# Late parts of u, squared chunks summed on GpSimd, a piecewise end and a chunk-wise start, in a four-layer decoder step

## The chip, the cores and the metric

The kernel runs on one core of one Trainium2 chip. The metric is the device time of one execution in microseconds (us). All times and rows here are of that one core.

## The reference, cut to what matters

One inference step of a decoder trunk. There are 1040 prompt columns and 32 sample columns, 1072 in all, each a vector of 1024 numbers. The trunk is: an attention and RWKV mixer, an MLP, a pooling mixer, an MLP. Each of the four is sandwiched between two RMS norms:

```
def rms_norm(x, g): return x * rsqrt(mean(x*x, -1) + 1e-6) * g
def channel_mixer(x, g_pre, g_post, w_up, w_down):      # the MLP, hidden width 4096
    h = rms_norm(x, g_pre)
    y = square(relu(h @ w_up)) @ w_down
    return x + rms_norm(y, g_post)
# pooling mixer: h = rms_norm(x); windows of 2, 4, 8, 16 columns, mean minus h,
#                a 256x256 product per group, then x + rms_norm(y, g_post)
```

The last MLP's x is the output y. Other outputs (latent rows, states) are written by stages that the change does not touch.

## The kernel before, in words

Features lie on the partitions, 128 at a time: x and y are tiles [128, 8 chunks, 1072 columns]. The columns are cut into three tiles of 358, 358 and 356. Products are made in float32r in three passes (`three_passes`, L222): weight and input are each split into a rounded head and a tail, and head*head, head*tail and tail*head are added up in PSUM.

**The first stage** (`project`, 20 slabs of w_in): ScalarE makes the heads of the input x chunk by chunk (L330), VectorE the tails (L395), GpSimd the tails of the weight slabs (L383). TensorE multiplies slab 0 with the column tiles 0, 1 and 2 in turn. Before each it waits for `x_tail`, which counts tiles: all eight chunks of that tile.

**The last stage** (`dense`) holds the output product (24 slots), the two MLPs and the pooling mixer between them. An MLP of one layer is two passes over its weights, the first for the column tiles 0 and 1, the second for tile 2 alone, so there are four passes of 64 slabs, 256 slabs of 512 KB. A pass has 8 blocks (fb) of 8 slabs, named here r0 to r7. r0 to r3 are up-slabs: 24 matmuls per column tile give 128 hidden rows in a PSUM bank; VectorE takes max(.,0)*rstd into `rl` (L2450), ScalarE squares it (L2274) and copies the rounded head into `u` (L2276), VectorE makes the tail (L2461, counter `u_tail`). r4 to r7 are down-slabs: each holds two output chunks (half 0 and 1) and multiplies all four parts of u, 12 matmuls per half and tile; VectorE adds the result to y (L2456; L2454 in the first block). Each slab is loaded by SP (L2021), its head is made by ScalarE (L2168) and its tail by VectorE (L2289) one slab ahead; there are two buffers, and the head of slab i+1 waits until TensorE is through slab i-1. A PSUM bank is written again only when VectorE has emptied it (`emptied`). One-tile slabs have 24 matmuls, two-tile slabs 48.

Each engine's program is written out by hand. Per slab i: ScalarE does head(i+1), `chains`, then the two activations of u; VectorE does tail(i+1), `chains`, then the emptying of slab i's products, then the tail of u; TensorE does slab i's products, then `chains`.

**The chains** are the norms, residuals and the pooling mixer. They hang on slots: job j of column tile t begins at slab start+o. A norm is: four squares of two chunks each (`square`, L2175, ScalarE, into sq[0] and sq[1] in turn), four `sums` (L2054, TensorE, 8 fp32 matmuls per part that the profile counts as 16), `root` (ScalarE), `invert` (VectorE, a reciprocal), `spread` (L2064, TensorE), and then `post` on VectorE: y times the rate (L2301) and x + y (L2308), two chunks a slot. `BETWEEN` places the four norms of one column tile between the two layers: POST_F (after the first MLP), PRE_M (before pooling), POST_M (after it), FFN1 (before the second MLP, with heads L2191 and tails L2321 of its input). Tile 0 starts at slab 65, tile 1 at 94 (both in the second pass, one tile a slab), tile 2 at 129 (third pass). `h_one`, `window_sums`, `pool` and `pool_product` (L2074) are the pooling mixer. `ENDING` places the last norm of tiles 0 and 1 in the fourth pass; that of tile 2 comes after slab 255. SP stores y in three pieces, one per column tile, each when its eight chunks are final; it also stores the pooling state (`pool_p`, `pool_s`) after it has issued slab 144.

The order of the work is fixed by these lists and the semaphores; there is no planner. GpSimd has no work in `dense`.

## Time and profile before

| | us |
|---|---|
| median of 3 timed runs (lowest, highest) | 3288.15 (3286.95, 3291.96) |
| the profiled execution: time | 3278.4 |
| its span | 3276.7 |
| TensorE matmuls busy | 2961.1 (90%) |
| VectorE busy | 1496.3 (46%) |
| ScalarE busy | 988.4 (30%) |
| GpSimd busy | 243.3 (7%) |

The span goes from the first to the last instruction of the profiled execution. The first stage lies before about 275 us, the last stage from 1436 us on; its four passes begin at about 1564, 2087, 2428 and 2972 us, and the last slab's products end at 3254. In a timeline row the second number is the length in us, `x24` is how many instructions the row merges, and the bracket is the idle time of the engine before the first of them, with what ended it. TensorE's granted clock (PEclk) is 1.00 at 2.4 GHz and 0.50 at 1.2 GHz.

### The profile page before, as it was taken

How to read it: one execution, taken by the hardware profiler on the slowest of the kernel's cores; microseconds unless marked ns; L12 is line 12 of the kernel's file. 1: busy time of each engine (PE TensorE's matmuls, PEld its weight loads, DVE VectorE, ACT ScalarE, POOL GpSimd, SP SyncE). 2: the span in 40 equal slices, each digit the busy share in tenths (PEclk: the TensorE clock that was granted, in tenths of full speed). 3: DMA queues.
4: the chain of work that ended last, by engine and by line, in shares of the span. 5: the costliest groups of instructions: out<-in, count | busy, mean ns of one | idle time of the engine just before them, and what ended most of it. 6: DMA issues, size and time to landing. Idle time of an engine off the chain costs nothing.

```text
span 3276.7 us, 70726 instructions
## 1 busy us (share of the span) xinstructions
PE 2961.1 (90%) x30941; PEld 2617.1 (80%) x30941; DVE 1496.3 (46%) x2569; ACT 988.4 (30%) x1817; POOL 243.3 (7%) x282
## 2 busy tenths in 40 slices
PE   7997888887888879989999999998999999999997
PEld 7996676664555556656999999988899899999896
DVE  3554444443343344413544434566655453445554
ACT  3102333321333334313322222334342232223332
POOL 1122222210000004300000000000000000000000
PEclk9997776866899889989999999999999999999998
DMA  3110000001000007730222222323342722223344
GB/s 121 40 39 28 5 4 4 4 5 57 1 8 10 0 13 233 220 124 1 78 65 68 68 65 65 90 90 98 97 97 65 59 65 65 65 65 97 116 123 131
DMA packets 92721, 216.85 MB, mean 66 GB/s; under 512 B 26833, under 2 KB 49778, under 8 KB 91666
## 3 DMA queue, kind: packets, MB, share of 16 engines
q1 hardware_dynamic: 86290, 193.71, 20.5%
q0 software_dynamic: 6144, 18.88, 1.9%
q8 instruction: 233, 3.82, 0.5%
q14 instruction: 54, 0.44, 0.0%
HBM read 205.11 MB, written 7.45 MB: 65 GB/s over the span
## 4 chain that ended last, share of the span: by engine, by line
PE 49%; DVE 4%; ACT 1%; DMA 1%; issue 1%; DVEq 0%; ACTq 0%
PE ps L222 44%; PE ps L2133 4%; PE ps L2074 1%; PE ps L2054 1%; DMA ds_raw<-w_mlp_dram 1%; DVE ds_rl L2450 1%; ACT ds_split L2168 1%; DVE ds_y L2301 1%; DVE ds_split L2289 1%; DVE ds_x L2308 1%; DVE ds_u L2461 0%; ACT ds_rl L2274 0%; PE ps L2064 0%; ACT ds_u L2276 0%; DVE ds_h L2321 0%
## 5 line engine op out<-in xcount | busy, mean ns | idle before, releaser
L222 PE MATMUL ps<-ds_u,ds_split 128*128 128x358 f32 (+1 forms) x4608 | 779.2, 330 | 57.1 <-DVE ds_u L2461 52.3
L222 PEld LDWEIGHTS ps<-ds_u,ds_split 128*128 128x128 f32 x4608 | 761.7, 190 | 69.7 <-issue 66.5
L222 PE MATMUL ps<-ds_h,ds_split 128*128 128x358 f32 (+1 forms) x4608 | 777.0, 328 | 4.2 <-DVE ds_y L2456 2.3
L222 PEld LDWEIGHTS ps<-ds_h,ds_split 128*128 128x128 f32 x4608 | 759.2, 189 | 13.1 <-issue 5.5
L2168 ACT CAST ds_split<-ds_raw 128x1024 fp32r<-128x1024 f32 x256 | 268.1, 1047 | 641.7 <-PE ps L222 623.3
L2289 DVE TENSOR_TENSOR ds_split<-ds_raw,ds_split 128x1024 fp32r<-128x1024 f32 x256 | 313.6, 1225 | 143.6 <-ACT ds_split L2168 143.5
L2456 DVE TENSOR_TENSOR ds_y<-ds_y,ps 128x358 f32<-128x358 f32 (+1 forms) x336 | 175.2, 524 | 281.9 <-PE ps L222 281.4
L222 PE MATMUL ps<-h,in_split 128*128 128x358 f32 (+1 forms) x1440 | 240.7, 328 | 16.8 <-DVE h L395 16.8
L222 PEld LDWEIGHTS ps<-h,in_split 128*128 128x128 f32 x1440 | 236.7, 189 | 18.3 <-issue 14.8
L2274 ACT ACTIVATE ds_rl<-ds_rl 128x358 f32<-128x358 f32 (+1 forms) x192 | 96.5, 503 | 497.9 <-DVE ds_rl L2450 497.9
L2450 DVE SCALAR_TENSOR_TENSOR ds_rl<-ps,ds_rstd 128x358 f32<-128x358 f32 (+1 forms) x192 | 101.5, 529 | 280.7 <-PE ps L222 277.2
L2461 DVE TENSOR_TENSOR ds_u<-ds_rl,ds_u 128x358 fp32r<-128x358 f32 (+1 forms) x192 | 101.3, 528 | 112.0 <-ACT ds_u L2276 112.0
L1441 PE MATMUL ps<-pa_PT,pa_V 128*64 128x128 f32 (+1 forms) x720 | 95.4, 280 | 60.4 <-DVE pa_PT L1546 42.1
L1441 PEld LDWEIGHTS ps<-pa_PT,pa_V 128*64 128x64 f32 x720 | 76.6, 145 | 78.5 <-issue 73.1
L1510 DVE TENSOR_REDUCE pa_mx<-ps 128x1 f32<-128x128 f32 (+8 forms) x72 | 58.3, 810 | 150.3 <-PE ps L1392 150.3
L2133 PE MATMUL ps<-z,ds_wout 128*128 128x358 f32 (+1 forms) x384 | 120.0, 471 | 4.3 <-DMA ds_wout<-w_out_dram 4.3
L1635 POOL DMA_DIRECT2D sa_C<-pool_dram x128 | 69.2, 541 | 579.1 <-issue 574.4
L2133 PEld LDWEIGHTS ps<-z,ds_wout 128*128 128x128 f32 x384 | 72.7, 192 | 45.7 <-DMA ds_wout<-w_out_dram 4.5
L2276 ACT CAST ds_u<-ds_rl 128x358 fp32r<-128x358 f32 (+1 forms) x192 | 94.4, 492 | 6.1
L1771 DVE COPY z<-ps 128x512 f32<-128x512 f32 (+1 forms) x80 | 51.0, 638 | 94.4 <-PE ps L1671 94.1
L1388 PE MATMUL ps<-pa_KT,pa_QT 96*128 96x512 f32 (+3 forms) x192 | 91.2, 589 | 0.0
L1671 PEld LDWEIGHTS ps<-const,sa_C 128*128 128x128 f32 x576 | 64.4, 144 | 29.8 <-issue 22.2
(326 smaller groups left out, 3330.5 us busy)
## 6 DMA issues: line engine op xcount, KB each, us to landing
ds_raw<-w_mlp_dram SPq DMA_DIRECT2D x256, 512.0 KB, 3.6
sa_C<-pool_dram SPq DMA_DIRECT2D x128, 144.0 KB, 3.1
sa_C<-pool_dram POOLq DMA_DIRECT2D x128, 144.0 KB, 3.3
in_raw<-w_in_dram SPq DMA_DIRECT2D x20, 512.0 KB, 3.6
ds_x<-xc_dram SPq DMA_DIRECT2D x1, 4288.0 KB, 18.8
ds_wout<-w_out_dram SPq DMA_DIRECT2D x8, 512.0 KB, 6.6
z<-xc_dram SPq DMA_DIRECT2D x2, 1432.0 KB, 9.6
y_dram<-ds_x SPq DMA_DIRECT2D x2, 1432.0 KB, 9.8
```

The source lines that it names most:

```text
L222: last = self.nc.tensor.matmul(out, w[:, a, k, m], rhs[:, b, rk, at:at + c], start=(start and n == 0), stop=(stop and n == 2))
L1388: mm(ps[0:n, bank + at // 512, 0:c], q, KT[:, e, at:at + c], start=True, stop=True)
L1441: last = mm(ps[rr(e), 6 + u % 2, 0:n], V[0:m, kb, rr(e)], PT[0:m, u % 2, kb, 0:n], start=(kb == 0), stop=(kb == i))
L1635: engine.dma_start(C[:, t % SLOTS, j:j + 1, :], io["pool"][bass.ds(page, 1)].rearrange("a p m -> p a m")).then_inc(pages_in[lane][t % SLOT ...
L2133: end = mm(ps[:, slot % 2, 0:wide(t)], wout[m][:, k, :], z[:, (Z_K + k if k < PAIRS else Z_R + k - PAIRS), cols(t)], start=(k == 0), stop= ...
L2168: nc.scalar.copy(split[i % 2][:, 0, :, :], raws[i % 2][:, :, :]).then_inc(g["slab_heads"].sem, 1)
L2274: nc.scalar.activation(rl[:, e % 2, 0:wide(n)], rl[:, e % 2, 0:wide(n)], ACT.Square).then_inc(g["u_squared"].sem, 1)
L2276: nc.scalar.copy(u[:, 0, r, u_cols(n)], rl[:, e % 2, 0:wide(n)]).then_inc(g["u_head"].sem, 1)
L2289: tt(split[i % 2][:, 1, :, :], raws[i % 2][:, :, :], split[i % 2][:, 0, :, :].bitcast(F32), ALU.subtract).then_inc(g["slab_tails"].sem, 1)
L2450: stt(out=rl[:, e % 2, 0:c], in0=ps[:, bank, 0:c], scalar=0.0, in1=rstd[:, cols(n)], op0=ALU.max, op1=ALU.mult).then_inc(g["emptied"].sem, 1)
L2456: tt(y[:, m, cols(n)], y[:, m, cols(n)], ps[:, bank, 0:c], ALU.add).then_inc(g["emptied"].sem, 1)
L2461: tt(u[:, 1, r, u_cols(n)], rl[:, e % 2, 0:wide(n)], u[:, 0, r, u_cols(n)].bitcast(F32), ALU.subtract).then_inc(g["u_tail"].sem, 1)
```

## The change

- **u late.** In the first down-slab of a block (r4) TensorE first runs the passes over the parts 0 to 2 of u for all halves and tiles (9 matmuls each), and only then, after waiting for the fourth part, the last 3 of each. In between, all banks stay open.
- **Sums between the layers.** For the 12 norms of `BETWEEN` (jobs 6 to 17) ScalarE squares part 0 into sq[0] and parts 1 to 3 into sq[1]; GpSimd adds the chunks (7 adds a job, 128 x 358 each), and TensorE makes one set of 4 matmuls where it made four sets of 8. ScalarE's squares of parts 2 and 3 wait for GpSimd's adds of the part before. The slots are spread out: tile 1 starts at slab 97 and tile 2 at 131, later steps come one to four slots later, and the pooling state is stored after slab 151.
- **The end.** TensorE runs the sums of the last norm's parts 0 to 2 behind the products of slabs 253, 254 and 255; ScalarE's squares for it stand behind its last head. GpSimd adds the odd chunks of x, VectorE the even ones, and SP stores tile 2 in four pieces of two chunks.
- **The start.** In slab 0 TensorE waits per chunk of x, not per tile.

The diff, cut to its core:

```diff
@@ project, tensor
-                            if m == 0:
-                                pe.wait_ge(g["x_tail"].sem, g["x_tail"].at(n + 1))
                             for k in range(KC):
+                                if m == 0:
+                                    pe.wait_ge(g["x_tail"].sem, g["x_tail"].at(KC * n + k + 1))
@@ dense
-        BETWEEN = {0: OUT_SLOTS + FIRST[0, 1] + 1, 1: OUT_SLOTS + FIRST[0, 1] + 30, 2: OUT_SLOTS + FIRST[1, 0] + 1}
+        BETWEEN = {0: OUT_SLOTS + FIRST[0, 1] + 1, 1: OUT_SLOTS + FIRST[0, 1] + 33, 2: OUT_SLOTS + FIRST[1, 0] + 3}
+        def by_pool(j):
+            return 6 <= j < 18
@@ sync
-                        if i == FIRST[1, 0] + 16:
+                        if i == FIRST[1, 0] + 23:
-                    for t in range(3):
+                    for t in range(2):
...
+                    for pair in range(KC // 2):
+                        sp.wait_ge(g["x_new"].sem, g["x_new"].at(KC * POST_NUMBER[LAST(2)] + pair + 1))
+                        sp.wait_ge(g["x_late"].sem, g["x_late"].at(pair + 1))
+                        sp.dma_start(io["y"][:, 2 * pair:2 * pair + 2, cols(2)], x[:, 2 * pair:2 * pair + 2, cols(2)]).then_inc(g["stored"].sem, 16)
@@ tensor, sums
+                        if by_pool(j):
+                            pe.wait_ge(g["added"].sem, g["added"].at(added_at(j, 3)))
+                            for q, at, c in quarters(wide(tile_of(j))):
+                                end = mm(ps[32 * q:32 * q + 32, 6, 0:c], self.c("ones", hi=32), sq[0][:, 0, at:at + c], start=True, stop=True)
+                            end.then_inc(g["summed"].sem, 1)
+                            return
@@ tensor, slots o of BETWEEN: before -> after
-  sums POST_F 0,1 (4 parts)  spread 2   sums PRE_M 4..7   spread 8   pool_product 11,13,15,17  sums POST_M 13,15,17,19  spread 20  sums FFN1 22..25  spread 26
+  sums POST_F 2 (one set)    spread 3   sums PRE_M 9      spread 10  pool_product 13,15,17,19  sums POST_M 22           spread 23  sums FFN1 29      spread 30
@@ tensor, products of a down-slab
+                            for k in range(UP - 1 if r == UP else UP):
+                                end = self.three_passes(ps[:, bank, 0:c], split[i % 2], UP * half + k, slice(0, P), u, k, u_cols(n).start, c, k == 0, k == UP - 1)
+                            if r > UP:
+                                end.then_inc(g["product"].sem, 1)
+                        if r == UP:
+                            for q, half, n, bank, before in uses[i]:
+                                if half == 0:
                                     pe.wait_ge(g["u_tail"].sem, g["u_tail"].at(up_number[i - 1, n] + 1))
+                                self.three_passes(ps[:, bank, 0:wide(n)], split[i % 2], UP * half + UP - 1, slice(0, P), u, UP - 1, u_cols(n).start, wide(n),
+                                                  False, True).then_inc(g["product"].sem, 1)
+                        if i >= N_SLABS - 3:
+                            sums(LAST(2), i - N_SLABS + 3)
                         chains(OUT_SLOTS + i)
-                    for o in range(3):
-                        ending(2, o)
+                    sums(LAST(2), 3)
+                    spread(LAST(2))
@@ scalar, square
+                        if part >= 2:
+                            if by_pool(j):
+                                act.wait_ge(g["added"].sem, g["added"].at(added_at(j, part - 1)))
+                        if by_pool(j) and part:
+                            nc.scalar.activation(sq[1][:, :, 0:wide(t)], src[:, 2 * part:2 * part + 2, cols(t)], ACT.Square).then_inc(g["squared"].sem, 1)
+                            return
@@ scalar, slots: PRE_M squares 4..7 -> 5..8, POST_M squares 13..19 -> 15..21, FFN1 heads and squares 22..25 -> 25..28; after the loop:
+                    for part in range(4):
+                        act.wait_ge(g["emptied"].sem, g["emptied"].at(done_slab(N_SLABS - 4 + part)))
+                        square(LAST(2), part, y)
+                    root(LAST(2))
@@ new
+                @block.gpsimd
+                def _(pool):
+                    add = nc.gpsimd.tensor_tensor
+                    for j in range(6, 18):
+                        c = wide(tile_of(j))
+                        for part in range(4):
+                            pool.wait_ge(g["squared"].sem, g["squared"].at(4 * j + part + 1))
+                            if part:
+                                pool.wait_ge(g["added"].sem, g["added"].at(added_at(j, part - 1)))
+                                add(sq[1][:, 0, 0:c], sq[1][:, 0, 0:c], sq[1][:, 1, 0:c], ALU.add).then_inc(g["added"].sem, 1)
+                                pool.wait_ge(g["added"].sem, g["added"].at(added_at(j, part) - 1))
+                            with_part = sq[1][:, 0, 0:c] if part else sq[0][:, 1, 0:c]
+                            add(sq[0][:, 0, 0:c], sq[0][:, 0, 0:c], with_part, ALU.add).then_inc(g["added"].sem, 1)
+                    n = POST_NUMBER[LAST(2)]
+                    for k in range(1, KC, 2):
+                        pool.wait_ge(g["scaled"].sem, g["scaled"].at(KC * n + k + 1))
+                        add(x[:, k, cols(2)], x[:, k, cols(2)], y[:, k, cols(2)], ALU.add).then_inc(g["x_late"].sem, 1)
@@ vector, post
+                            if j == LAST(2) and k % 2:
+                                continue
@@ vector, slots: POST_F post 3..6 -> 4..7, h_one 9..12 -> 11..14, windows 10,12,14,16 -> 12,14,16,18, pool 11,13,15,17 -> 13,15,17,19, POST_M post 21..24 -> 24..27, FFN1 tails 22..25 -> 25..28
```

## Rows read from the trace of the kernel before

**Rows 1.** The four passes as stretches: length, busy PE PEld DVE ACT POOL, PEclk, DMA share, GB/s.
```profile
1560.00:2087.00 527.00, 516.87 (x3228) 511.57 (x3227) 221.10 (x347) 138.10 (x211) 0.00 (x0) 1.00 0.22 69
2087.00:2427.50 340.50, 310.77 (x2178) 288.78 (x2177) 221.09 (x338) 135.82 (x200) 0.00 (x0) 0.96 0.32 98
2427.50:2971.50 544.00, 533.03 (x3394) 521.33 (x3393) 250.17 (x424) 147.63 (x228) 0.00 (x0) 0.99 0.31 66
2971.50:3255.00 283.50, 261.76 (x1683) 254.87 (x1681) 159.00 (x226) 100.97 (x138) 0.00 (x0) 0.99 0.41 124
```

**Rows 2.** Waits: who waited for whom, us in total, times, longest.
```profile
PE ps L222 <- DVE ds_u L2461: 52.3, 31, 4.1
```

**Rows 3.** Timeline, a two-tile pass, where up turns to down (start, length, idle before).
```profile
1732.64 4.53 PE L222 MATMUL ps<-ds_u,ds_split 128*128 128x358 f32 x26 [1.15 <-DVE ds_u L2461]
```

**Rows 4.** Timeline, a one-tile pass, where up turns to down.
```profile
3168.11 0.53 DVE L2450 SCALAR_TENSOR_TENSOR ds_rl<-ps,ds_rstd 128x356 f32<-128x356 f32 x1
...
3170.41 15.78 PE L222 MATMUL ps<-ds_u,ds_split 128*128 128x356 f32 x96 [2.33 <-DVE ds_u L2461]
...
3170.68 1.23 DVE L2289 TENSOR_TENSOR ds_split<-ds_raw,ds_split 128x1024 fp32r<-128x1024 f32 x1 [0.42 <-ACT ds_split L2168]
...
3172.61 0.53 DVE L2456 TENSOR_TENSOR ds_y<-ds_y,ps 128x356 f32<-128x356 f32 x1 [0.71 <-PE ps L222]
```

**Rows 5.** Timeline, two down slabs of the second pass, one sums part between.
```profile
2287.85 4.14 PE L222 MATMUL ps<-ds_u,ds_split 128*128 128x356 f32 x24
...
2292.37 4.14 PE L222 MATMUL ps<-ds_u,ds_split 128*128 128x356 f32 x24
```

**Rows 6.** One line's instructions (min/median/max ns), and one GpSimd instruction of the timeline.
```profile
L1285 POOL TENSOR_TENSOR rw_bonus_v<-rw_bonus_v,rw_lnb x9: 1260/1288/1350, 310.2 to 713.5; 128x512 f32<-128x512 f32 x8, 64x512 f32<-64x512 f32 x1
...
L395 DVE SCALAR_TENSOR_TENSOR h<-z,vec,h x24: 577/586/2352, 10.6 to 25.9; 128x358 fp32r<-128x358 f32 x16, 128x356 fp32r<-128x356 f32 x8
...
20.22 2.41 POOL L383 TENSOR_TENSOR in_split<-in_raw,in_split 128x1024 fp32r<-128x1024 f32 x1 [10.09 <-ACT in_split L324]
```

**Rows 7.** Timeline and one stretch, second pass, where updates of x crowd VectorE.
```profile
2122.74 1.08 DVE L2301 SCALAR_TENSOR_TENSOR ds_y<-ds_y,vec,ps 128x358 f32<-128x358 f32 x2
...
2123.96 0.97 DVE L2308 TENSOR_TENSOR ds_x<-ds_x,ds_y 128x358 f32<-128x358 f32 x2
...
2221.61 0.52 DVE L2450 SCALAR_TENSOR_TENSOR ds_rl<-ps,ds_rstd 128x356 f32<-128x356 f32 x1
...
2228.43 0.52 DVE L2450 SCALAR_TENSOR_TENSOR ds_rl<-ps,ds_rstd 128x356 f32<-128x356 f32 x1
...
2281.94 5.53 PE L222 MATMUL ps<-ds_u,ds_split 128*128 128x356 f32 x24 [4.07 <-DVE ds_u L2461]
...
2141.00:2152.00 11.00, 6.93 (x30) 6.66 (x29) 8.47 (x14) 2.77 (x4) 0.00 (x0) 0.69 0.33 100
```

**Rows 8.** DMA issues (KB, us to landing) and timeline, third pass, rows of the pooling state.
```profile
pool_s_dram<-ds_full SPq DMA_DIRECT2D x1, 480.0 KB, 32.1
...
2576.27 1.04 ACT L2168 CAST ds_split<-ds_raw 128x1024 fp32r<-128x1024 f32 x1 [15.36 <-DMA ds_raw<-w_mlp_dram]
```

**Rows 9.** Timeline and DMA issues, the end.
```profile
3254.82 2.92 ACT L2175 ACTIVATE ds_sq<-ds_y 128x712 f32<-128x712 f32 x4 [7.22 <-DVE ds_y L2456]
...
3261.95 1.08 DVE L2301 SCALAR_TENSOR_TENSOR ds_y<-ds_y,vec,ps 128x356 f32<-128x356 f32 x2 [2.11 <-PE ps L2064]
...
3268.79 0.97 DVE L2308 TENSOR_TENSOR ds_x<-ds_x,ds_y 128x356 f32<-128x356 f32 x2
...
y_dram<-ds_x SPq DMA_DIRECT2D x1, 1424.0 KB, 6.4
```

**Rows 10.** Timeline, the start.
```profile
14.83 9.79 PE L222 MATMUL ps<-h,in_split 128*128 128x358 f32 x48 [14.83 <-DVE h L395]
...
20.67 5.85 DVE L395 SCALAR_TENSOR_TENSOR h<-z,vec,h 128x356 fp32r<-128x356 f32 x8 [1.96 <-ACT h L330]
...
26.58 8.10 PE L222 MATMUL ps<-h,in_split 128*128 128x356 f32 x48 [1.95 <-DVE h L395]
```

More of the change, by code:

```diff
@@ L462, in _ @@
                     chain.close()
-            for n, events in (("product", 3 * NZ), ("emptied", 3 * NZ), ("slab_heads", NZ), ("slab_tails", NZ), ("loaded", 16), ("late_in", 64), ("x_head", 3 * KC), ("x_tail", 3)):
+            for n, events in (("product", 3 * NZ), ("emptied", 3 * NZ), ("slab_heads", NZ), ("slab_tails", NZ), ("loaded", 16), ("late_in", 64), ("x_head", 3 * KC), ("x_tail", 3 * KC)):
                 g[n].passed(events)
@@ L1946, in dense, with added_at @@
         PREPARED = {(layer, t): 3 * layer + t for layer in range(2) for t in range(3)}
+        def by_pool(j):
+            return 6 <= j < 18
+        events = [0]
+        for j in range(21):
+            events.append(events[-1] + (1 if by_pool(j) else 4))
+        ADDS = 7
+        def added_at(j, part):
+            return ADDS * (j - 6) + 2 * part + 1
         def cols(t):
@@ L2424, in chains @@
-                            if 22 <= o < 26:
-                                tails(1, t, range(2 * (o - 22), 2 * (o - 22) + 2))
+                            if 11 <= o < 15:
+                                h_one(t, range(2 * (o - 11), 2 * (o - 11) + 2))
+                            if o in (12, 14, 16, 18):
+                                windows[t] = window_sums(t, (o - 12) // 2)
+                            if o in (13, 15, 17, 19):
+                                pool(t, (o - 13) // 2, *windows[t])
@@ L2426, in chains @@
+                            if 25 <= o < 29:
+                                tails(1, t, range(2 * (o - 25), 2 * (o - 25) + 2))
                         for t, start in ENDING.items():
```

115 lines of the change are left out of this document (51 added, 64 removed).

## The prediction

> **What bounds the kernel now.** I read the busy time by stretch first, since the change touches four places that have different limits. In all four MLP passes TensorE is the engine that sets the time, at a granted clock near 1.00: it is busy for 516.9 of 527, 310.8 of 340.5, 533.0 of 544 and 261.8 of 283.5 us [rows 1]. So in the passes with two tiles little is left to gain beside work taken off TensorE, and in the passes with one tile 30 and 22 us are idle. The view of waits says for what: 52.3 us, in 31 waits, for the last tail of u, by far the longest item of TensorE [rows 2]. There is one such wait in each of the 32 blocks. In a two-tile pass it is 1.15 us [rows 3], in an undisturbed one-tile pass 2.33 us [rows 4], in the second pass up to 4.07 us [rows 7].
>
> Why it is 2.33: the last up-product ends just before VectorE's 3168.11 row; then come VectorE, two activations and VectorE again, until TensorE starts at 3170.41 [rows 4]. Meanwhile ScalarE and VectorE prepare the next slab: its tail runs from 3170.68 to 3171.91. This loop (empty the bank, two activations, head, tail) is some 3.85 us long against 24 matmuls of 15.78/96 = 0.164 us, 3.94 us. So in one-tile up-slabs TensorE and the loop are tied: whatever delays VectorE or ScalarE there comes out as a stall, and in two-tile slabs (twice as long) it does not.
>
> **Part 1, u late, two tiles (passes 1 and 3).** 36 matmuls (5.9 us) now stand ahead of the first use of u's last part, so the wait of 1.15 us goes. What is late next? The next slab's tail is ready some 3.9 us after the last up-product, and the first bank's last 3 matmuls end 1.5 us before the slab's end, while VectorE needs 0.53 us to empty it: nothing. 16 blocks x 1.15 = 18.4 us gained.
>
> **Part 2, u late, one tile.** 18 matmuls (2.95 us) cover the 2.33. But now r4 ends at about 3168.07 + 3.94 = 3172.0, half 0 and half 1 end 0.5 us apart at its very end, and r5 needs half 0's bank. On VectorE the tail of the next slab stands ahead of the emptying and lasts till 3171.91; then 0.53 us of emptying: r5 starts at 3172.55, against 3170.41 + 3.94 = 3174.35 before. 1.8 us a block are gained, 0.5 lost to the new wait. In pass 4 six blocks are like this; in the first two the post of tiles 0 and 1 stands in r4 on VectorE (2.1 us, as in [rows 7]) ahead of the emptying, and eats nearly all of it: 0.5 each. Pass 4: 6 x 1.8 + 1 = 12 us.
>
> **Part 3, sums.** One part of sums between two slabs makes 4.52 us from start to start [rows 5] where 3.94 is the slab: 0.6 us a part. Of 4 parts per norm one set of half the size stays (0.45 us by that row: most of it is the change-over); where two parts stood together (POST_F) the change-over was shared. I count 7 us per column tile (four norms: 1.5, 1.9, 1.8, 1.8), 21 for all. For tile 2 in pass 3 nothing else is near the limit: 7 us.
>
> **Part 4, the pooling state's store.** Its transfer takes 32.1 us and the weight slab behind it came so late that ScalarE idled 15.36 us waiting for a DMA [rows 8]; at TensorE this cost some 5 us beside the slow clock after it. Moved from slab 144 to 151, it goes out while slab 148 is worked on; between then and the need for slab 152 lie two slabs with a pooling product, as before one and a half. I take 4 us gained (bounds: 0, if the slab is as late as before, and 7).
>
> **Part 5, pass 2 (tiles 0 and 1 between the layers, one tile a slab).** Gained: u late 8 x 1.8 = 14 us; sums 14 us, but not all of it counts. Where x is updated, VectorE needs 1.23 (slab tail) + 1.08 + 0.97 [rows 7] + 2 x 0.53 = 4.3 us a down-slab, more than TensorE's 3.94: the sums of PRE_M and FFN1 stood in that shadow. I keep 8 us. Tile 1's first update (slots 97 to 100, which are r1 to r4) ended in the wait of 4.07 us and a stretch on the slow clock (5.53 us for 24 matmuls) [rows 7]; it moves to r5, r6, r7 and r0, which I put at 4 us gained.
> Lost: (a) POST_M's update and FFN1's heads, squares and tails move from r6, r7, r0, r1 (tile 0) and r3 to r6 (tile 1) to r1 to r5 for both. There the loop is 0.53 + 1.0 + 1.05 + 1.23 + 2.05 + 1.1 us, about 7, which the trace shows: 6.82 us between two L2450 with both in between [rows 7]. TensorE then stalls some 1 + 3 + 2 us in r2 to r4, and in r5 once more (4 us), because VectorE has not emptied r4's banks: some 11 us a tile, with the clock lowered after each longer stall; a window with such a wait stood at 0.69 between the levels of 1.2 and 2.4 GHz (0.50 and 1.00) [rows 7], so 13. Today the two tiles lose about 4 each by the same count. Net 9 a tile, 18 us. (b) In POST_F, ScalarE's fourth square waits for the two adds of the third. An add of 128 x 358: one of 512 columns takes 1.29 us, one of 1024 takes 2.41 [rows 6], a slope of 1.12 per 512, so 0.95 us. Two adds are 1.9 us in front of an up-slab's activations: 1.8 us x 2 tiles = 3.5 us. (c) The adds against VectorE: a VectorE instruction with both inputs in SBUF took 2352 ns in place of 586 when GpSimd's 2.41 us instruction had begun 0.45 us before it [rows 6]; it waited for the end. 56 adds of 0.95 us in this pass; where they come, VectorE spends about a third of its time in such forms (slab tails, u tails, x + y), so a third of them hit, half an add each, and half of that reaches TensorE: 56 x 1/3 x 0.47 x 1/2 = 4 us; bounds 0 and 56 x 0.95 = 53. I round (a) to (c) to 23 to 25 us against 26 gained. To this comes that the pooling windows meet up-slabs a little more kindly (the 4 us window no longer in r1 but in r3, where 0.5 us of slack now lies): 3. Net 5 us gained; this is the least certain term, and I give it -12 to +26.
> The Trainium skill, "SBUF — State Buffer", section "Who interferes with whom", says that a VectorE instruction with two SBUF inputs and a GpSimd one that reads SBUF shut each other out for their whole length. By that rule, the trace agrees (2352 ns against 586), and with every add on the path it would turn the sum as in the last rival.
>
> **Part 6, the end.** After the last product: emptying, 4 squares (2.92 us from 3254.82), sums, root, spread, post from 3261.95, the last x + y ending at 3269.76, a store of 1424 KB that lands in 6.4 [rows 9]. Now three squares leave that line: 2.2 us gained. But square 0 stands on ScalarE behind head(255), which waits for the products of slab 253, and TensorE's sums behind slab 253 wait for it: 0.05 + 1.05 + 0.8 + 0.1 = 2.0 us of stall, and two parts of sums at 0.6 are now in line: 3.2 us lost. Post: VectorE drops 4 x 0.48 = 1.9 us, GpSimd's last add ends 0.95 after it; the last of four stores is a quarter: the three quarters before it (at 360 GB/s 3 us) are gone. 1.9 - 0.95 + 3 = 4 us gained. End: 3 us (0 to 5).
>
> **Part 7, the start.** TensorE now follows the tails chunk by chunk. Tile 2's tails end at 20.67 + 5.85 = 26.52, and its 24 matmuls were then all to come [rows 10]; now 3 are: 21 x 0.163 = 3.4 us. What comes behind it (sums, root) waits on TensorE, not on a load. 3.4 us (bounds 0 and 3.9).
>
> **Sum.** 18.4 + 12 + 7 + 4 + 5 + 3 + 3.4 = 53 us. 3278.4 - 53 = 3225 for an execution like the profiled one. The median of the timed runs is 3288.15, 10 us above it; I take the difference off the median: 3235 us.
>
> **Rivals.**
> A. The later slots cost nothing in pass 2 (ScalarE and VectorE catch up in the slack that u late opens). For it: tile 0's update of today, half of it in up-slabs, loses only some 4 us. Against: the 6.82 us loop. (a) falls to nothing: 53 + 18 = 71, 3217 us.
> B. Pass 2 is crowded more than I count, because each stall brings the slow clock and the locks hit in the same slots: 20 us more, 3255 us.
> C. The wait for u's last part is replaced in full, by the bank that r5 needs or by the next slab's tail. For it: the tail ends only 0.1 us before r4 does [rows 4]. Against: the same row ends it in time. Then 18.4 + 14 + 12 = 44 go, and 9 are left: 3279 us.
> D. Slower than before: the lock between GpSimd and VectorE. 84 adds in `BETWEEN`, 0.95 us each; if each pushed VectorE back by its whole length on the path, 80 us, less the 4 counted: 3235 + 76 = 3311 us. It decides from 0.67 us on the path per add (57/84). Against: a third of the adds fall into pass 3, where VectorE is busy for 250 of 544 us [rows 1] and has time to give, and most of its work in pass 2 reads PSUM and one tile only.
>
> **Chances.** Forecast 0.52, A 0.19, B 0.16, C 0.06, D 0.05, and 0.02 that it all cancels. Within 0.2% means within 6.6 us, about what a measurement of this kernel can tell from no change. Faster: forecast, A, B and C but for its upper end: 0.92. Same: 0.03. Slower: 0.05. The forecast's own range is 3220 to 3250; with A's and B's centres, the term of pass 2 (-12 to +26) and the bounds of parts 4, 6 and 7 it is 3206 to 3264.
>
> **What would show it.** Waits of TensorE for L2461 gone in passes 1, 3 and 4, and in pass 4 r4 plus r5 with a wait of about 0.5 us for the bank (L2456). Passes 1 to 4 shorter by 9, 5, 20 and 12 us. In pass 2 L2450 at distances of 5.5 to 7 us in slots 89 to 92 and 121 to 124 with waits of TensorE for VectorE of 2 to 4 us in r4 and r5. A TensorE stall of 2 us behind slab 253 for ScalarE's square. The last store landing in 3.3 us. GpSimd's adds at 0.95 us; single L2308 or L2289 lengthened by up to that. It would be wrong if pass 2 (340.5 us) came out shorter than 320 or longer than 350 us, or if passes 1 and 3 kept a wait at r4 or r5.

## The result: 3238.82 us against 3287.55, and the profile after

Timed beside each other, the changed kernel takes 3238.82 us (median of 4 runs, 3234.22 to 3243.11) and the kernel before 3287.55 (3286.38 to 3291.96): a ratio of 0.9849 with an interval of 0.9831 to 0.9867, or 48.7 us less. 3235 was forecast. In the profiled executions it is 3234.22 against 3278.4 us, 44.2 less, where the sum of the prediction has 53.

The four MLP passes and the stretch after slab 252, by the view of windows (us; columns as in [rows 1]: length, busy us and count of PE, PEld, DVE, ACT and POOL, granted clock, DMA share, GB/s):

```profile
1565.80:2079.00 513.20, 511.44 (x3216) 509.95 (x3217) 220.29 (x346) 137.59 (x210) 0.00 (x0) 1.00 0.22 70
2079.00:2415.50 336.50, 299.49 (x1729) 277.67 (x1727) 234.01 (x338) 136.55 (x201) 60.52 (x56) 0.96 0.32 99
2415.50:2946.50 531.00, 523.78 (x3171) 518.57 (x3170) 254.77 (x425) 147.03 (x228) 30.47 (x28) 0.99 0.33 67
2946.50:3219.00 272.50, 263.13 (x1731) 253.97 (x1729) 158.31 (x226) 103.44 (x141) 0.00 (x0) 1.00 0.41 129
```

The first pass has 1.8 us of idle left in 513, so it stands at what its matmuls need. The second pass still has 37 us idle, more than before (30), although it is shorter: what was taken off TensorE there did not all come off the time.

TensorE's waits from 1500 us to the end (us in total, times, longest):

```profile
PE ps L222 <- DVE ds_y L2511: 21.9, 17, 7.2
PE ps L2094 <- DVE ds_y L2436: 9.6, 5, 3.0
PE ps L222 <- DVE ds_split L2342: 8.8, 8, 2.7
PE ps L222 <- DVE ds_y L2509: 5.7, 5, 1.8
PE ps L222 <- DVE ds_rl L2505: 4.7, 2, 2.6
PE ps L2074 <- ACT ds_sq L2208: 2.9, 2, 1.9
```

The item of 52.3 us for u's last tail [rows 2] is gone (its line would be L2516). In its place stand waits for a bank to be emptied (L2511), for the next slab's tail (L2342) and for the windows of the pooling (L2436): 53.6 us in these six rows, of which the first five have 34.8 in the second pass, and the longest single wait, 7.2 us, stands in the third.

For what follows I cut each profile at the start of the first product of slabs 0, 64, 128, 192 and 252 (starts of L222 in the timeline) and take the differences. "Start" runs to the beginning of the last projection product of the first stage; "middle" is the stretch between it and slab 0, in which all kernels here are the same.

| kernel | start | middle | pass 1 | pass 2 | pass 3 | pass 4 to slab 252 | from there to the end |
|---|---|---|---|---|---|---|---|
| before | 271.0 | 1293.4 | 522.9 | 340.4 | 544.0 | 266.8 | 38.2 |
| changed | 267.1 | 1298.6 | 513.2 | 336.6 | 531.1 | 251.7 | 34.2 |
| changed, second profile (e11) | 267.8 | 1290.6 | 513.2 | 336.7 | 528.3 | 251.6 | 34.5 |
| e1 only u late | 271.1 | 1303.4 | 513.2 | 329.2 | 534.6 | 251.5 | 37.6 |
| e2 old slots, TensorE sums | 267.3 | 1301.8 | 514.8 | 329.9 | 533.1 | 251.5 | 33.8 |
| e3 new slots, TensorE sums | 268.2 | 1308.6 | 514.8 | 326.3 | 535.7 | 251.5 | 35.9 |
| e4 old slots, GpSimd adds | 267.1 | 1304.2 | 513.3 | 348.7 | 529.5 | 251.5 | 34.3 |
| e5 pool_s in pieces | 266.8 | 1289.0 | 513.2 | 335.8 | 520.9 | 251.6 | 35.2 |
| e6 square first | 267.3 | 1284.1 | 514.8 | 333.4 | 527.9 | 251.4 | 31.7 |
| e7 adds doubled | 267.1 | 1295.7 | 513.3 | 354.4 | 528.2 | 251.4 | 35.2 |
| e8 GpSimd for tile 2 only | 269.1 | 1287.4 | 513.3 | 326.6 | 528.3 | 251.5 | 34.6 |
| e9 e8 + pieces + square first | 267.2 | 1299.4 | 514.8 | 328.9 | 520.9 | 251.6 | 31.7 |
| e10 e9 + GpSimd in two norms | 267.0 | 1303.3 | 514.8 | 323.8 | 520.9 | 251.5 | 32.1 |

This table says how far a single profile can be trusted. The middle, in which no kernel differs, runs from 1284 to 1309 us, so whole times of single executions differ by up to 25 us for nothing; the passes repeat to some 3 us (e11 against the changed kernel: 0.0, 0.1, 2.8, 0.1; pass 2 of e3, e8 and e9, which have the same order in it: 326.3, 326.6, 328.9; pass 2 of the changed kernel's order in its two profiles, e5 and e6: 336.6, 336.7, 335.8, 333.4). The two values of pass 1, 513.2 and 514.8, differ in one slab, the sixth (8.8 or 10.3 us), for a reason not looked into. The steps are judged by the passes. Changed against before they give -3.9, -9.7, -3.8, -12.9, -15.1 and -4.0, together -49.4; the middle gave 5.2 back.

### The profile page after: what moved, and what is told of

The parts are those of the page before. It is cut to its first block, busy times and chain, and to the rows that moved or that the text cites. A ratio compares the mean times of both kernels' runs of the same rounds, so it can differ in the third digit from the quotient of the medians.

```text
span 3232.5 us, 69489 instructions
## 1 busy us (share of the span) xinstructions
PE 2944.9 (91%) x30269; PEld 2605.6 (81%) x30269; DVE 1512.2 (47%) x2565; ACT 988.2 (31%) x1817; POOL 338.7 (10%) x370
## 3 DMA queue, kind: packets, MB, share of 16 engines
q1 hardware_dynamic: 86338, 193.71, 20.6%
## 4 chain that ended last, share of the span: by engine, by line
PE 46%; DVE 4%; ACT 2%; issue 1%; DMA 1%; POOL 0%; ACTq 0%; DVEq 0%; POOLq 0%
PE ps L222 41%; PE ps L2150 4%; ACT ds_split L2195 1%; DVE ds_split L2342 1%; DMA ds_raw<-w_mlp_dram 1%; PE ps L2094 1%; DVE ds_y L2354 1%; DVE ds_x L2363 1%; ACT ds_rl L2307 1%; PE ps L2084 1%; DVE ds_rl L2505 1%; PE ps L2074 0%; DVE ds_h L2376 0%; DVE ds_wa L2415 0%; DVE ds_y L2511 0%
## 5 line engine op out<-in xcount | busy, mean ns | idle before, releaser
L222 PE MATMUL ps<-ds_u,ds_split 128*128 128x358 f32 (+1 forms) x4608 | 779.5, 329 | 30.9 <-DVE ds_y L2511 14.3
L222 PEld LDWEIGHTS ps<-ds_u,ds_split 128*128 128x128 f32 x4608 | 760.6, 190 | 42.7 <-issue 21.6
L222 PE MATMUL ps<-ds_h,ds_split 128*128 128x358 f32 (+1 forms) x4608 | 776.4, 328 | 10.9 <-DVE ds_y L2511 7.6
L222 PEld LDWEIGHTS ps<-ds_h,ds_split 128*128 128x128 f32 x4608 | 759.7, 189 | 20.1 <-DVE ds_split L2342 13.5
L2342 DVE TENSOR_TENSOR ds_split<-ds_raw,ds_split 128x1024 fp32r<-128x1024 f32 x256 | 315.1, 1231 | 144.6 <-ACT ds_split L2195 144.6
L2511 DVE TENSOR_TENSOR ds_y<-ds_y,ps 128x358 f32<-128x358 f32 (+1 forms) x336 | 171.8, 524 | 235.8 <-PE ps L222 234.6
L222 PE MATMUL ps<-h,in_split 128*128 128x358 f32 (+1 forms) x1440 | 241.7, 329 | 12.0 <-DVE h L395 12.0
L222 PEld LDWEIGHTS ps<-h,in_split 128*128 128x128 f32 x1440 | 237.4, 190 | 13.8 <-POOL in_split L383 10.9
L2505 DVE SCALAR_TENSOR_TENSOR ds_rl<-ps,ds_rstd 128x358 f32<-128x358 f32 (+1 forms) x192 | 101.5, 529 | 264.6 <-PE ps L222 257.5
L2327 POOL TENSOR_TENSOR ds_sq<-ds_sq 128x358 f32<-128x358 f32 (+1 forms) x48 | 54.4, 1134 | 993.8 <-ACT ds_sq L2208 991.0
L2516 DVE TENSOR_TENSOR ds_u<-ds_rl,ds_u 128x358 fp32r<-128x358 f32 (+1 forms) x192 | 102.2, 532 | 115.3 <-ACT ds_u L2309 115.3
## 6 DMA issues: line engine op xcount, KB each, us to landing
ds_x<-xc_dram SPq DMA_DIRECT2D x1, 4288.0 KB, 18.8
```

What stands on the lines that cost most here:

```text
L222: last = self.nc.tensor.matmul(out, w[:, a, k, m], rhs[:, b, rk, at:at + c], start=(start and n == 0), stop=(stop and n == 2))
L2342: tt(split[i % 2][:, 1, :, :], raws[i % 2][:, :, :], split[i % 2][:, 0, :, :].bitcast(F32), ALU.subtract).then_inc(g["slab_tails"].sem, 1)
L2505: stt(out=rl[:, e % 2, 0:c], in0=ps[:, bank, 0:c], scalar=0.0, in1=rstd[:, cols(n)], op0=ALU.max, op1=ALU.mult).then_inc(g["emptied"].sem, 1)
L2511: tt(y[:, m, cols(n)], y[:, m, cols(n)], ps[:, bank, 0:c], ALU.add).then_inc(g["emptied"].sem, 1)
L2516: tt(u[:, 1, r, u_cols(n)], rl[:, e % 2, 0:wide(n)], u[:, 0, r, u_cols(n)].bitcast(F32), ALU.subtract).then_inc(g["u_tail"].sem, 1)
```

## The experiments

**e1, u late alone.** The kernel before, with only TensorE's order in r4 changed:

```diff
-                                for k in range(UP):
+                            for k in range(UP - 1 if r == UP else UP):
...
+                                self.three_passes(..., UP * half + UP - 1, slice(0, P), u, UP - 1, ..., False, True).then_inc(g["product"].sem, 1)
```

> The kernel before with the late use of u's last part alone. Theory: the wait of 1.15 us goes in the 16 two-tile blocks and 1.8 us net in the one-tile blocks, so passes 1 and 3 lose 9 to 10 us each, pass 4 12 to 15, pass 2 14 or more, 50 us in all: about 3237. Rival (a new wait takes its place where ScalarE and VectorE are crowded): pass 2 moves by less than 6 us, and the sum is 35 to 40 us, about 3250.

Measured: 3245.32 us (3242.21 to 3246.00) against 3280.22, ratio 0.9896 (0.987 to 0.9921). By passes 9.7, 11.2, 9.4 and 15.3 us, 45.6 in all; the 35 of the medians hold the unsteady middle too. Passes 1 and 4 are where the whole change has them, so nothing else of the change acts there. Pass 2 gains 11.2: below the 14 that the prediction and the theory had, and above the 6 of the rival. It is 7.4 us more than the whole change gains there (4.3 by e6's profile of the same pass). What the change adds to pass 2 beside this is therefore a loss.

**e2 and e3, slots and sums apart.** e2 is the changed kernel with the old slots of `BETWEEN` (and the pooling state's store behind slab 144) and TensorE's four parts of sums; e3 keeps the new slots and the new place of the store, with TensorE's sums.

```diff
-            return 6 <= j < 18
+            return False
...
-        BETWEEN = {0: OUT_SLOTS + FIRST[0, 1] + 1, 1: OUT_SLOTS + FIRST[0, 1] + 33, 2: OUT_SLOTS + FIRST[1, 0] + 3}
+        BETWEEN = {0: OUT_SLOTS + FIRST[0, 1] + 1, 1: OUT_SLOTS + FIRST[0, 1] + 30, 2: OUT_SLOTS + FIRST[1, 0] + 1}
```

The first two lines are in both, the last two in e2 alone; the slots of the single steps, which follow from them, are left out here.

> The changed kernel without anything between the layers: TensorE makes all sums, in the slots of before, the pooling state is stored after slab 144. u late, the end and the start stay. Theory (the spread-out slots cost in pass 2 what the sums taken off TensorE give, and the later store costs 3 to 4 us in pass 3): pass 2 within 5 us of the changed kernel's 336.6, pass 3 longer than its 531.1 by 7 us of sums less 3.5 of the store, 534 to 535; whole time within 6 us of the changed kernel's 3239. Rival (GpSimd's adds carry a good part of the gain): pass 2 and 3 together longer by 15 us or more, 3255.

> The changed kernel with its new slots, but TensorE makes all sums, in four parts, and GpSimd adds none. Theory: in pass 3 the 7 us of sums come back whole (531.1 to 538); in pass 2 only what did not stand in VectorE's shadow, 8 us, less what GpSimd's adds cost there (the wait of ScalarE in POST_F 3.5 us and lengthened VectorE instructions 10 us in sum, about half on the path): within 4 us of the changed kernel's 336.6. Rival (the adds are free and the sums count in full): pass 2 longer by 12 to 14 us, about 350. Rival (the lock weighs more than the sums): pass 2 shorter by 5 us or more.

Measured: e2 3232.42 us, ratio 0.9854 (0.9828 to 0.9881); e3 3227.03 (3219.11 to 3242.84), ratio 0.9831 (0.9802 to 0.986). In whole times neither can be told from the changed kernel; in pass 2 both can: 329.9 and 326.3 against 336.6 (333.4 to 336.7 in the four profiles with this pass 2). e2 was to stay within 5 us of it and e3 within 4; both are shorter by more, and for e3 that is its second rival, by which the lock weighs more than the sums. So the expected net loss by the new slots is not there, and GpSimd's adds, which I had as a gain, cost 10 us with the new slots (5 to 10 over all profiles of the two orders).

**e4, old slots with GpSimd's adds,** for the three norms whose old slots leave them time:

```diff
-            return 6 <= j < 18
+            return 6 <= j < 18 and (j - 6) % 4 > 0
```

> The changed kernel with the slots of before; GpSimd adds the squares of three of the four norms between the layers (PRE_M, POST_M, FFN1), TensorE keeps POST_F's sums, the pooling state is stored after slab 144. Theory (the new slots put POST_M's update and FFN1's heads and tails of both tiles into up-slabs, at 9 us a tile): pass 2 shorter than the changed kernel's 336.6 by 10 to 18 us, about 322; whole time about 3225. Rival (the crowd is the same wherever it stands): pass 2 within 5 us of 336.6.

Measured: 3245.35 us (3237.82 to 3250.22), ratio 0.9887 (0.9859 to 0.9916); pass 2 at 348.7, longer by 12.1 than the changed kernel, where my theory had it shorter. That refutes the theory outright: with GpSimd's adds the new slots are better by 12.1 us; with TensorE's sums they are no worse (e3, e8 and e9 have 326.3 to 328.9, e1 and e2, the two kernels with the old slots, 329.2 and 329.9: 0.3 to 3.6 us, hardly more than the passes repeat to). The adds cost 5 to 10 us in the new slots (56 adds) and 18.8 in the old (42 adds). TensorE's waits in pass 2, first of e3, then of the changed kernel, then of e4:

```profile
PE ps L222 <- DVE ds_y L2514: 7.6, 7, 2.7
PE ps L2074 <- ACT ds_sq L2211: 7.5, 6, 2.0
PE ps L2094 <- DVE ds_y L2439: 3.1, 4, 1.2
```

```profile
PE ps L222 <- DVE ds_y L2511: 10.3, 8, 3.8
PE ps L2094 <- DVE ds_y L2436: 9.6, 5, 3.0
PE ps L222 <- DVE ds_split L2342: 8.8, 8, 2.7
PE ps L222 <- DVE ds_rl L2505: 4.7, 2, 2.6
```

```profile
PE ps L222 <- DVE ds_y L2512: 14.3, 8, 4.1
PE ps L2094 <- DVE ds_y L2437: 11.3, 6, 3.2
PE ps L2068 <- POOL ds_sq L2328: 9.5, 3, 6.1
```

With TensorE's sums, 7.5 us are waits for ScalarE's squares; with GpSimd's adds these are gone and VectorE is late instead, in its windows, tails and emptying. In e4 TensorE waits for GpSimd itself on top.

**e5, the pooling state's store in eight pieces,** one chunk of 60 KB behind each of eight slabs:

```diff
+                        if FIRST[1, 0] + 20 <= i < FIRST[1, 0] + 28:
+                            k = i - FIRST[1, 0] - 20
...
+                            sp.dma_start(io["pool_s"][:, k], full[:, k, :, DS:KEPT + DS]).then_inc(g["pool_out"].sem, 16)
...
-                            sp.dma_start(io["pool_s"], full[:, :, :, DS:KEPT + DS]).then_inc(g["pool_out"].sem, 16)
```

> The changed kernel with the pooling state's store cut into eight pieces, one behind each of the weight slabs 148 to 155, in place of one transfer after slab 151. Theory (the one transfer of 8192 small rows holds up the weight slab behind it): slabs 151 and 152 of pass 3 take 15.5 and 10.7 us in the changed kernel and 7.9 to 8.0 here, pass 3 shorter by 8 to 10 us, 522. Rival (the small rows cost the same wherever they stand, since each piece of some 4 us delays its slab): the loss is spread over slabs 149 to 156 and pass 3 stays within 3 us of 531.1.

Measured: 3214.19 us in one run, beside 3277.76 of the kernel before. Pass 3 takes 520.9 us, 10.2 less than in the changed kernel's first profile, 7.4 less than in its second and 7.0 less than in e6. Issues (KB each, us to landing) and ScalarE's wait, changed kernel, around slab 151:

```profile
pool_s_dram<-ds_full SPq DMA_DIRECT2D x1, 480.0 KB, 35.0
...
2622.20 1.04 ACT L2195 CAST ds_split<-ds_raw 128x1024 fp32r<-128x1024 f32 x1 [20.63 <-DMA ds_raw<-w_mlp_dram]
...
2625.09 16.16 PE L222 MATMUL ps<-ds_h,ds_split 128*128 128x358 f32 x80 [7.22 <-DVE ds_y L2511]
```

and the same issue in e9, which stores it in the same pieces:

```profile
pool_s_dram<-ds_full SPq DMA_DIRECT2D x8, 60.0 KB, 6.5
```

In e5 ScalarE has no wait for a DMA in this stretch. Slabs 151 and 152 took 15.52 and 10.72 us in the changed kernel and take 8.15 and 7.92, which is the 10.2 us of the pass. The other 62 slabs of the pass take 504.84 us in the changed kernel, in e11, in e6 and in e5 alike: all that differs between profiles of this pass stands in these two slabs. The row of TensorE names VectorE's emptying, but VectorE waited for ScalarE and ScalarE for the load: the releaser named last isn't the cause.

**e6, the square of part 0 ahead of the last head:**

```diff
+                        if i == N_SLABS - 2:
+                            act.wait_ge(g["emptied"].sem, g["emptied"].at(done_slab(N_SLABS - 4)))
+                            square(LAST(2), 0, y)
                         if i + 1 < N_SLABS:
                             head(i + 1)
```

> The changed kernel with ScalarE's first square of the last norm ahead of its last head, head(255). Theory (TensorE waits behind slab 253 for a square that stands behind that head): slab 253 takes 6.46 us in the changed kernel and 4.5 here, the end as a whole 1.9 to 2.0 us less. Rival (the wait is for the emptying of y or for the sums themselves): slab 253 stays above 6 us, or slab 254 takes what 253 gives.

Measured: 3212.39 us in one run. The changed kernel, then e6, behind slab 253:

```profile
3208.00 1.48 ACT L2208 ACTIVATE ds_sq<-ds_y 128x712 f32<-128x712 f32 x2
...
3208.84 0.52 PE L2074 MATMUL ps<-ds_sq,late_const 128*32 128x90 f32 x16 [1.89 <-ACT ds_sq L2208]
```

```profile
3184.24 0.80 ACT L2208 ACTIVATE ds_sq<-ds_y 128x712 f32<-128x712 f32 x1
...
3187.55 0.52 PE L2074 MATMUL ps<-ds_sq,late_const 128*32 128x90 f32 x16
```

The wait of 1.89 us is gone, and slab 253 takes 4.50 us in place of 6.46; slab 254, which the rival had taking the gain back, has 4.52 against 4.53. The stretch to the end is 31.7 us against 34.2 and 34.5 in the two profiles of the changed kernel.

**e7, more adds on GpSimd:** six further operations of the same size per norm, the result left alone.

```diff
-        ADDS = 7
+        ADDS = 13
...
+                                for more in range(2):
+                                    pool.wait_ge(g["added"].sem, g["added"].at(added_at(j, part) - 3 + more))
+                                    add(sq[0][:, 1, 0:c], sq[0][:, 1, 0:c], sq[0][:, 1, 0:c], ALU.subtract).then_inc(g["added"].sem, 1)
```

> The changed kernel with 13 GpSimd operations per norm between the layers in place of 7: after each of parts 1 to 3 two more of the same size on a chunk that nobody reads. Theory (GpSimd's work between the layers costs in pass 2 by making ScalarE wait and by locking VectorE's two-input instructions out, some 10 us for 56 operations): pass 2 longer by 8 to 15 us (48 more operations), 345 to 350, with L2363 lengthened about twice as often; pass 3 longer by less than 4 us. Rival (the cost of GpSimd's part is the change-over to its semaphores and the later sums, not its busy time): pass 2 within 3 us of 336.6.

Measured: 3246.98 us in one run. Pass 2 is 17.8 us longer, more than the 8 to 15 of my theory; pass 3, where VectorE has time, is none longer (528.2). But the growth is not what I had it for. Whole profile of e7, who waited for its second adds, and then the changed kernel's:

```profile
L2330 POOL TENSOR_TENSOR ds_sq<-ds_sq x48: 813/1112/1817, 2083.4 to 2702.5; 128x358 f32<-128x358 f32 x32, 128x356 f32<-128x356 f32 x16
...
  ACT ds_sq L2206: 19.9, 9
...
  PE ps L2068: 15.3, 4
```

```profile
L2327 POOL TENSOR_TENSOR ds_sq<-ds_sq x48: 813/1106/1807, 2086.5 to 2688.9; 128x358 f32<-128x358 f32 x32, 128x356 f32<-128x356 f32 x16
...
  ACT ds_sq L2206: 7.2, 4
...
  PE ps L2068: 1.3, 2
```

ScalarE and TensorE wait 12.7 and 14.0 us longer for GpSimd, a chain of waits, while VectorE's x + y (of L2363 in the changed kernel) was lengthened 25 times against 19, not twice as often. By blocks of eight slabs the growth stands in the two blocks of POST_F (first 36.9 to 44.2, fifth 36.9 to 46.0), so e7 measures another place than the one where the unchanged adds cost time.

**e8, GpSimd's adds for tile 2 alone** (pass 3), TensorE's sums for tiles 0 and 1, new slots:

```diff
-            return 6 <= j < 18
+            return 14 <= j < 18
```

> The changed kernel where GpSimd adds only the squares of tile 2 (in the two-tile pass 3); TensorE makes the sums of tiles 0 and 1 in four parts, in the new slots. Theory (the adds pay where a slab is 8 us and cost where it is 4): pass 2 as with TensorE's sums alone, 326 (326.3), pass 3 as in the changed kernel, 531: 10 us less than the changed kernel in the sum of the passes. Rival (what pass 2 gained came from something else in that kernel, or pass 3 depends on how pass 2 leaves the queues): pass 2 above 332 or pass 3 above 534.

Measured: 3212.38 us in one run; pass 2 at 326.6, as e3, and pass 3 at 528.3, 7.4 below e3's 535.7. The adds gain in the pass with two tiles and lose in that with one.

**e9, what the runs point to:** e8, e5 and e6 together. **e10:** e9 with GpSimd also for POST_F and PRE_M of tiles 0 and 1. **e11:** the changed kernel once more, unchanged.

The edit of e10 against e9:

```diff
+        ADDED = (6, 7, 10, 11, 14, 15, 16, 17)
...
-            return 14 <= j < 18
+            return j in ADDED
```

> The changed kernel with three edits at once: TensorE makes the sums of tiles 0 and 1 (GpSimd adds for tile 2 alone), the pooling state's store goes out in eight pieces, the first square of the last norm stands ahead of head(255). Theory (the three gains add up, since they lie in three stretches): pass 2 at 326, pass 3 at 521, 2.0 us less at the end, so 20 to 22 us less than the changed kernel over these stretches, and 70 less than the kernel before: about 0.979 of it. Rival (they overlap, or the untouched attention stage gives it back): less than 12 us below the changed kernel in the passes.

> As the one with the three edits, but GpSimd also adds the squares of POST_F and PRE_M of tiles 0 and 1; their POST_M and FFN1 sums stay on TensorE. Theory (GpSimd costs where VectorE does windows, updates of x and FFN1's tails, that is at POST_M and FFN1, and pays a little at PRE_M): pass 2 at 324 to 326. Rival (GpSimd costs wherever it works beside a one-tile pass, by the wait in POST_F): pass 2 at 330 or more.

> The changed kernel once more, beside the two others. Theory: the passes repeat to within 3 us (513.2, 333 to 337, 528 to 531, about 271) and the stretch between the first stage and the MLP passes, which no edit touches, moves by 5 us or more against its 1298.6 of the first profile; ratio to the kernel before 0.983 to 0.987. Rival (that stretch is set by the changed start): it stays within 2 us of 1298.6.

Measured: e9 3210.75 us (3207.38 to 3216.24), ratio 0.9789 (0.9768 to 0.981); e10 3212.82 (3204.12 to 3216.72), 0.9796 (0.9772 to 0.982); e11 3226.79 (3224.40 to 3239.85), 0.9858 (0.9832 to 0.9884). e9 lies 16 us below the changed kernel's 3226.79 beside it, and the ranges don't overlap; it beats both kernels. In pass 2, pass 3 and the end it has 20.3 us less than the changed kernel's first profile and 18.0 less than e11, where 20 to 22 were expected: the three gains add up. Between e9 and e10 the whole time can't tell. e11's middle is 8.0 us shorter than in the first profile of the same kernel, so what moves it isn't an edit. Pass 2 is 328.9 us in e9 (326 expected) and 323.8 in e10 (324 to 326 expected); windows of e9 and e10:

```profile
2081.43:2410.34 328.91, 305.57 (x2177) 282.98 (x2177) 220.01 (x338) 136.32 (x201) 0.00 (x0) 0.98 0.32 101
```

```profile
2085.03:2408.82 323.79, 298.51 (x1954) 275.97 (x1953) 223.17 (x338) 136.53 (x201) 29.71 (x28) 0.99 0.34 103
```

Here the blocks show that the difference of 5.1 us isn't all that of the edit. Block by block (us of eight slabs, pass 2):

| | 1 | 2 | 3 | 4 | 5 | 6 | 7 | 8 |
|---|---|---|---|---|---|---|---|---|
| before | 38.3 | 45.3 | 46.5 | 41.4 | 42.5 | 48.0 | 41.9 | 36.6 |
| changed | 36.9 | 37.6 | 48.8 | 47.1 | 36.9 | 37.6 | 43.4 | 48.3 |
| e3 TensorE sums | 36.7 | 38.4 | 43.5 | 44.8 | 36.8 | 38.3 | 42.8 | 45.1 |
| e7 adds doubled | 44.2 | 38.0 | 45.5 | 49.5 | 46.0 | 37.7 | 43.6 | 49.8 |
| e9 | 36.6 | 38.4 | 43.5 | 46.4 | 36.7 | 38.3 | 42.7 | 46.2 |
| e10 | 36.9 | 37.6 | 43.5 | 45.1 | 36.9 | 37.6 | 42.7 | 43.5 |

POST_F and PRE_M lie in blocks 1, 2, 5 and 6: 150.1 us in e3, e8 and e9, 149.0 in e10 and 149.0 or 149.1 in the four profiles of the changed kernel's order, so their 28 adds gain 1 us. The rest of the 5.1 stands in blocks 4 and 8, in which e9 and e10 don't differ: it is spread. POST_M and FFN1 lie in blocks 3, 4, 7 and 8: 176.2 us in e3, 178.8 in e9, 174.8 in e10, all with TensorE's sums, against 187.6 in the changed kernel, 186.7 in e5 and 184.4 in e6. Their 28 adds cost 6 to 13 us, in the blocks where windows, tails of h and x + y also need VectorE.

## Why the prediction came out near, and where it was wrong

The median was right to 4 us, and that is in part luck: the same kernel's median was 12 us lower in e11 (3226.79), and errors cancelled in part. Against the sum of 53, pass 3 gave 7 less and pass 2 1 less; pass 1, pass 4, start and end together gave 5 more; the untouched middle took 5. That makes the 44 of the profiles.

- **Part 1, u late, two tiles: right.** 18.4 forecast, 9.7 and 9.4 (e1) measured. The wait of 1.15 us is gone, and TensorE runs on through the turn:

```profile
1731.38 10.85 PE L222 MATMUL ps<-ds_u,ds_split 128*128 128x358 f32 x65
```

- **Part 2, one tile, pass 4: right in mechanism, 3 us small.** The undisturbed blocks went from 34.0 to 32.2 us, the 1.8 of the working; the first two gained 1.1 and 1.2 where I had 0.5, and the third, which still has work of the norm behind it, 3.3. Forecast 12, measured 15.1. The new wait for r5's bank (rival C's) stands there at 0.31 us, behind VectorE's emptying:

```profile
3169.92 0.95 DVE L2511 TENSOR_TENSOR ds_y<-ds_y,ps 128x356 f32<-128x356 f32 x2
...
3170.59 5.58 PE L222 MATMUL ps<-ds_u,ds_split 128*128 128x356 f32 x33 [0.31 <-DVE ds_y L2511]
```

- **Part 3, sums of tile 2: right.** 7 us forecast. e3's pass 3 is 4.6 to 7.8 us longer than those with the adds and the store in one piece; without slabs 151 and 152, which the store disturbs, it is 511.84 against 504.84 us, 7.0.
- **Part 4, the pooling state's store: wrong in sign.** Forecast 4 us gained, bounds 0 to 7. The transfer took 35.0 us (32.1 before), ScalarE waited 20.63 us for the load behind it (15.36 before, [rows 8]). By slabs: with the store behind 144, ScalarE waits 15.1 to 16.0 us and slab 144 takes 15.5 to 17.3 us, where slab 146 with the same product of the pooling takes 10.0 to 10.7, so 5 to 7 are lost (before, e1, e2, e4). With the store behind 151, ScalarE waits 18.2 to 20.6 us and slabs 151 and 152 take 23.1 to 26.2 us together, 7 to 10 more than the 16.1 of e5 (changed, e3, e6, e7, e8, e11). On average that is 6.0 us lost before and 7.8 behind the move: some 2 us more, where I had 4 gained. The failed step is "between then and the need for slab 152 lie two slabs with a pooling product, as before one and a half": I gave the later place more time, but what decides is that the load queued behind the 480 KB lands only after them, some 35 us after the issue, and by then the slabs in hand (8 us each) are used up. Neither of the two places that ran escapes that; e5's pieces do.
- **Part 5, pass 2: the total near, the split wrong.** Forecast 5 gained, measured 3.8. The terms:
  - The terms as they stand add up to 3.5, not 5: 26 gained and 3 for the windows, less (a), (b) and (c), 18 + 3.5 + 4 = 25.5, which I rounded to 23 to 25. That 3.8 was measured is chance, as the next lines show.
  - u late 14: e1 shows 11.2.
  - (a) later slots, 9 a tile lost, less 4 and 3 for tile 1's first update and the windows, net 11 lost: e1 and e2 against e3, e8 and e9 show 0 to 4 gained. The mechanism in the up-slabs was there: L2505 stands at 2219.05 and 2226.64, 7.59 us apart where I had about 7, with the stalls behind it:

```profile
2222.88 1.72 PE L222 MATMUL ps<-ds_u,ds_split 128*128 128x356 f32 x9 [2.65 <-DVE ds_split L2342]
...
2227.22 3.86 PE L222 MATMUL ps<-ds_u,ds_split 128*128 128x356 f32 x15 [2.62 <-DVE ds_rl L2505]
...
2234.89 5.36 PE L222 MATMUL ps<-ds_u,ds_split 128*128 128x356 f32 x22 [3.82 <-DVE ds_y L2511]
```

In e3, without the adds, the five slabs 89 to 93 take 3.98, 5.70, 6.58, 9.38 and 5.82 us, 31.5 against 5 times 4.0: some 11 us a tile, near my 13. To see the other side I took pass 2 apart by the steps of tiles 0 and 1: the time of a step's slabs less that of the same slabs in an undisturbed block (the fifth of pass 4: 34.0 us before, 32.2 with u late). The three steps are slabs 64 to 73, 74 to 84 and 85 to 93 of tile 0 and 94 to 102, 103 to 113 and 114 to 127 of tile 1 in the old slots; 64 to 75, 76 to 87, 88 to 96 and 97 to 107, 108 to 119, 120 to 127 in the new.

| us, tiles 0 and 1 | POST_F and PRE_M | pooling | POST_M's update and FFN1 |
|---|---|---|---|
| before, old slots | 16.0 | 33.6 | 18.5 |
| e1 and e2, old slots | 20.2, 19.0 | 34.5, 32.9 | 16.8, 20.4 |
| e3, e8, e9, new slots | 14.4, 14.3, 14.3 | 28.7, 28.8, 28.6 | 25.6, 25.9, 28.2 |
| changed, e11, e6, e5, new slots and adds | 13.2 each | 34.6, 34.8, 31.7, 33.9 | 31.0, 31.0, 30.9, 30.8 |

The last column in the new slots is 13 to 14 a tile, as I had it (TensorE's sums, 2.4 us a tile by the 0.6 of the prediction, stand in it, in the old slots too). In the old slots it is 8 to 10 a tile where I had 4 "by the same count": that is the failed step, the price of the old slots, and it was as wrong in the kernel before (9 a tile) as with u late. So the move costs 5 to 11 us there, not 18. The other side, 4 for tile 1's first update and 3 for the windows, was nearly right: 5 to 6 and 4 to 6.
  - Sums off TensorE 8 gained, (b) 3.5 and (c) 4 lost, so about 0: 5 to 10 lost in the new slots, and 18.8 in the old. (b) is small: ScalarE waited 4.9 us in three squares. (c) was sized at half an add for a third of the adds, half of which reaches TensorE; both counts came out too small. VectorE's and GpSimd's instructions at 2223.74; x + y of two chunks takes 0.97 us where it is undisturbed [rows 7]:

```profile
2223.74 1.98 DVE L2363 TENSOR_TENSOR ds_x<-ds_x,ds_y 128x358 f32<-128x358 f32 x2
2224.22 1.10 POOL L2327 TENSOR_TENSOR ds_sq<-ds_sq 128x358 f32<-128x358 f32 x1
...
2235.60 1.81 POOL L2327 TENSOR_TENSOR ds_sq<-ds_sq 128x358 f32<-128x358 f32 x1
2236.53 1.77 DVE L2376 SCALAR_TENSOR_TENSOR ds_h<-ds_x,vec,ds_h 128x358 fp32r<-128x358 f32 x2
```

In pass 2 VectorE is busy for 234.0 us with the adds and for 220.0 with TensorE's sums (the window rows of the changed kernel and of e9), with the same instructions: 14.0 us longer, where the working has 56 x 1/3 x 0.47 = 8.8. And more than half of it seems to reach TensorE: the pass lost 5 to 10 us although TensorE has some 5 us less to do (299.5 us busy against 304.1 in e3). The 14.0 us would about cover both if all of it came out; but VectorE isn't on the path all the time, and one delay can hold up several engines.
That the two engines shut each other out is the rule of the Trainium skill, "SBUF — State Buffer", section "Who interferes with whom"; the trace agrees in the lengths (1.98 against 0.97 us for VectorE, 1.81 against 0.82 for GpSimd).
That the lock makes these 5 to 10 us is argued, from the lengths and from the steps in which they stand. The granted clock of the pass is lower too, 0.96 against 0.98 in e3; no run took the lock away and left the adds, and how much is lock, chain of waits and clock stays open.
- **Part 6, the end: right, 1 us small.** 3 forecast, 4.0 measured. The stall behind slab 253 was there at 1.89 us (2.0 forecast). From the end of the last product to that of the span it is 14.6 us where it was 22.4, 7.9 less (6.2 forecast); the stores of 356 KB land in 2.5 us (1424 KB in 6.4, [rows 9]):

```profile
y_dram<-ds_x SPq DMA_DIRECT2D x4, 356.0 KB, 2.5
```

The final x + y of VectorE is 1.25 us, beside GpSimd's last add, where its three fellows are 0.52.

```profile
3226.72 0.52 DVE L2363 TENSOR_TENSOR ds_x<-ds_x,ds_y 128x356 f32<-128x356 f32 x1
...
3228.32 0.93 POOL L2331 TENSOR_TENSOR ds_x<-ds_x,ds_y 128x356 f32<-128x356 f32 x1 [0.28 <-DVE ds_y L2354]
3228.38 1.25 DVE L2363 TENSOR_TENSOR ds_x<-ds_x,ds_y 128x356 f32<-128x356 f32 x1
```

- **Part 7, the start: right.** 3.4 forecast, 3.9 measured: the first product starts at 10.91 us (14.83, [rows 10]), and the third tile's wait fell from 1.95 to 1.09.

```profile
10.91 10.63 PE L222 MATMUL ps<-h,in_split 128*128 128x358 f32 x48 [10.91 <-DVE h L395]
...
22.64 8.21 PE L222 MATMUL ps<-h,in_split 128*128 128x356 f32 x48 [1.09 <-DVE h L395]
```

Of the rivals, A (the later slots cost nothing) is what happened to the slots in sum, though not because they cost nothing: they cost 5 to 11 us in one step, and the two steps before it gave that back; C didn't come (0.31 us of it); D's lock is real in pass 2 but nowhere near its whole length for each add, and costs nothing in pass 3; B's crowding came with the adds, not from the slots. Pass 2 came to 336.6, between the 320 and 350 that I had named as the points of failure, which shows that a right total proved none of its terms: only the runs that took them apart did.
